# A 31-tap convolution rebuilt as column-tiled matmuls, its norm and the attention reordered ahead of a scan

## The reference, cut to what matters

```python
h = rms_norm(x, norm_mix_g); p = h @ w_in                       # (256, 2560)
q, pc, pr = split(p, [256, 256 + 768])
# cross attention to 256 memory rows, 4 heads of 64
s = einsum('qhd,mhd->hqm', q, mem_n @ w_mk) * 64 ** -0.5
o_att = einsum('hqm,mhd->qhd', softmax(s), mem_n @ w_mv)
# convolution: 384 channels, each with its own 31 taps along the tokens
val, gate = split(pc, 2)
u = conv(val * sigmoid(gate), conv_w, padding=15, groups=384) + conv_b
u = (u - mean(u)) * rsqrt(var(u) + 1e-5) * ln_g + ln_b          # over the 384 channels
o_conv = silu(u)
# RWKV: a scan in both directions over 6 heads of 64, in chunks of 32 tokens
y = scan_forward + scan_backward
y = (y - mean_head(y)) * rsqrt(var_head(y) + 64e-5) * lnx_g + lnx_b
o_rwkv = (y + sum_d sum_head(r * k_d * r_k) * v) * g            # the sum is the bonus
x = x + concat([o_att, o_conv, o_rwkv]) @ w_out                 # then 16 experts
```

## Time and profile before

| | |
|---|---|
| median of 3 runs | 1893.52 us |
| the profiled execution | 1893.73 us, its span 1891.9 us |
| PE busy, of the span | 1494.6 us (79%) |
| DVE, ACT, POOL busy | 464.9, 301.7, 95.1 us |
| the mixing stage, from its first matmul (h3T) to its last (output projection) | 1105.5 to 1376.8 us |
| of it, the scan | 1225.9 to 1333.7 us |
| the 16 experts and the end | 1377 to 1891.9 us |

### The profile page before, as it was taken

How to read it: one execution, slowest core, us unless ns; L and a number is a source line. 1 busy time by engine, 2 the same in 40 slices (tenths; PEclk the granted TensorE clock), 3 DMA queues, 4 the chain that set the end, 5 groups by cost and what they waited for, 6 DMA issues and landing times.

```text
span 1891.9 us, 25668 instructions
## 1 busy us (share of the span) xinstructions
PE 1494.6 (79%) x10943; PEld 850.7 (45%) x10943; DVE 464.9 (25%) x953; ACT 301.7 (16%) x666; POOL 95.1 (5%) x194
## 2 busy tenths in 40 slices
PE   6999988889896888888888769577857676766764
PEld 2845866778344343432343258366532131321321
DVE  1011234220016222212222253677530000000002
ACT  1101223440001111111111103221111010100100
POOL 3000021000000000000000000022000000000000
PEclk8999999889888899999999979677869798988978
DMA  9772362123664699999999772000238999999995
GB/s 353 166 262 80 112 223 95 55 79 112 226 244 156 280 428 428 429 430 427 429 430 427 303 269 91 0 3 4 90 144 356 429 428 427 430 428 428 429 429 231
DMA packets 84764, 510.29 MB, mean 270 GB/s; under 512 B 9527, under 2 KB 12376, under 8 KB 60118
## 3 DMA queue, kind: packets, MB, share of 16 engines
q1 hardware_dynamic: 80950, 500.21, 64.9%
q0 software_dynamic: 3744, 9.06, 2.1%
HBM read 506.10 MB, written 3.15 MB: 269 GB/s over the span
## 4 chain that ended last, share of the span: by engine, by line
PE 58%; DMA 24%; DVE 8%; issue 6%; ACT 3%; POOL 0%; SPq 0%; POOLq 0%; DVEq 0%; ACTq 0%; PEldq 0%
PE ps L1168 47%; DMA ring<-in_w_e_up 15%; DMA ring<-in_exp_w 7%; PE ps L1593 4%; PE ps L1730 3%; DVE hTs L2458 1%; DMA brow<-in_ada_b 1%; DMA ring<-in_ada_w 1%; DVE arena L2370 1%; PE ps L1578 1%; ACT arena L951 1%; DMA arena<-in_causal 1%; PE ps L1200 1%; ACT arena L941 1%; DVE stats L2058 0%
## 5 line engine op out<-in xcount | busy, mean ns | idle before, releaser
L1168 PE MATMUL ps<-ring,arena 128*32 128x512 f32 (+2 forms) x3492 | 483.0, 667 | 145.5 <-DMA ring<-in_w_e_up 81.8
L1168 PEld LDWEIGHTS ps<-ring,arena 128*32 128x32 f32 (+1 forms) x3492 | 133.4, 125 | 441.3 <-issue 376.0
L1168 PE MATMUL ps<-hTs,ring 128*128 128x256 f32 (+2 forms) x1120 | 249.9, 384 | 3.3 <-PE ps L1168 3.3
L1168 PEld LDWEIGHTS ps<-hTs,ring 128*128 128x128 f32 (+2 forms) x1120 | 210.9, 190 | 42.2 <-issue 11.5
L1168 PE MATMUL ps<-arena 128*128 (+5 forms) x576 | 139.5, 398 | 2.4 <-POOL arena L654 2.4
L1593 PE MATMUL ps<-arena 128*128 128x512 f32 x256 | 117.5, 601 | 29.0 <-DVE arena L2370 29.0
L1168 PEld LDWEIGHTS ps<-arena 128*128 128x128 f32 (+1 forms) x576 | 123.0, 294 | 18.9 <-issue 11.2
L1168 PE MATMUL ps<-ring,hTs 128*128 128x512 f32 (+2 forms) x288 | 106.2, 523 | 5.8 <-ACT hTs L1099 5.8
L1593 PEld LDWEIGHTS ps<-arena 128*128 128x128 f32 x256 | 46.0, 189 | 103.0 <-ACT arena L953 57.1
L2370 DVE COPY arena<-ps 128x512 f32<-128x512 f32 x32 | 22.1, 691 | 249.2 <-PE ps L1168 249.2
L2713 DVE TENSOR_TENSOR arena<-arena,ps 64x512 f32<-64x512 f32 x16 | 11.0, 690 | 292.1 <-ACT arena L1123 292.1
(11 more groups left out here) (423 smaller groups left out, 1235.1 us busy)
## 6 DMA issues: line engine op xcount, KB each, us to landing
ring<-in_exp_w SPq DMA_DIRECT2D x96, 2048.0 KB, 18.6
ring<-in_w_e_gate SPq DMA_DIRECT2D x32, 2048.0 KB, 18.8
ring<-in_w_e_up SPq DMA_DIRECT2D x32, 2048.0 KB, 23.3
ring<-in_w_e_down SPq DMA_DIRECT2D x32, 2048.0 KB, 24.0
ring<-in_w_in SPq DMA_DIRECT2D x22, 2048.0 KB, 14.1
ring<-in_ada_w SPq DMA_DIRECT2D x12, 2048.0 KB, 13.3
ring<-in_w_out SPq DMA_DIRECT2D x4, 2048.0 KB, 12.4
ring<-in_w_br_hg SPq DMA_DIRECT2D x2, 2048.0 KB, 15.4
```

The costliest lines, as they stand in the source:

```text
L1168: return nc.tensor.matmul(o, lhsT, rhs, start=start, stop=stop)
```

## The change

1. **Order of the projection.** The fourth weight tile (queries and two value groups) is kept, and the fifth (`in2b`, third value group and gates) goes first; what is left of the fourth comes behind `vt` as the jobs `ca` (values) and `qa` (queries), with the head sums of the bonus in between.
2. **Convolution on PE.** POOL multiplies `CU`, SP makes 16 DMAs from it into `lags`: the input of 32 channels in four copies, shifted by 0 to 3 tokens, on 128 partitions, for each of 12 groups. POOL builds `taps`, blocks of 128x32 with the taps on diagonals. A group is then 8 matmuls (shifts by 4) with 128x32 weights and 256 columns; four groups lie beside each other in one bank. The 93 DVE instructions go away.
3. **Its norm ahead of the scan.** ACT adds the bias while it empties the banks; the two channel sums `CM` and `CR` stand between the attention's jobs, POOL centres and squares, ACT takes the root, and DVE divides within the first pair of the scan, behind the four levels.
4. **Attention.** All four score jobs come first, each head has its own buffers; ACT's exponential reads the bank itself and scales by 0.125, and DVE only reduces and negates.
5. **Bonus** on POOL, straight after the low-rank results; `k_a` and `r_k` are folded into two column vectors by DVE.
6. **Behind the scan** PE goes to `gn1` at once, `project(0, 1)`, `gn2`, then `project(1, 5)`. ACT takes the root straight out of the bank with the epsilon as its bias. The scale and shift of the head norm are folded into `GG` and `BON` within the first pair, so that two products and one sum are left of it.

The diff, cut to its core:

```diff
-PLAN2 = [("h3T", 4), ("in2", 8), ("w0", 2), ("w1", 2), ("gg", 2), ("a0", 2), ("a1", 2),
-         ("kks", 2), ("vt", 2), ("in2b", 2), ("matt", 10), ("bon", 2), ("cmean", 1),
-         ("gn1", 2), ("y2", 4), ("cvar", 1), ("gn2", 2), ...
+PLAN2 = [("h3T", 4), ("in2", 6), ("in2b", 2), ("w0", 2), ("w1", 2), ("gg", 2), ("a0", 2), ("a1", 2),
+         ("kks", 2), ("vt", 2), ("ca", 1), ("bon", 2), ("qa", 1), ("matt", 14),
+         ("gn1", 2), ("y2", 4), ("gn2", 2), ...
-        ATT = ("S0", "S1", "T0", "S2", "T1", "O0", "S3", "T2", "T3", "O1")
+        ATT = ("S0", "S1", "S2", "S3", "C0", "C1", "T0", "T1", "CM", "T2", "O0", "T3", "CR", "O1")
@@ SP, ahead of the experts' first tiles
+            sp.wait_ge(S("cu_ready"), 1)
+            for j in range(4):
+                for q in range(4):
+                    sp.dma_start(lags[32 * j:32 * j + 32, q::4, :], CU[32 * q:32 * q + 32, :, j:j + 284])\
+                        .then_inc(S("lags_loaded"), 16)
@@ POOL
+            pool.wait_ge(freed[(N2 - 1) % RING], free_count(N2 - 1 - RING))
+            for j in range(4):
+                for q in range(4):
...
+                    ins = nc.gpsimd.tensor_copy(b, a)
...
+            for i, (o, n) in enumerate(((0, 40), (40, 56))):
+                ins = ptt(taps[i], mid(msk("eye32"), n), last(tapc[:, o:o + n], CHUNK), ALU.mult)
...
+            ptt(BON, AA[0], AA[1], ALU.add).then_inc(S("bonus_terms"), 1)
...
+            for c in range(3):
+                ins = nc.gpsimd.tensor_scalar(BON[:, c, :], BON[:, c, :], kark[:, c:c + 1], c2rk[:, c:c + 1],
+                                              ALU.mult, ALU.add)
...
+            ptt(BON, BON, K_, ALU.mult).then_inc(S("bonus_terms"), 1)
...
+            ptt(BON, BON, R_, ALU.mult).then_inc(S("bonus_terms"), 1)
...
+            is_out(pool, J("ca"))
+            all_out(pool, "in2b", 2)
+            ptt(CU[:, :, 15:271], CA, CS, ALU.mult).then_inc(S("cu_ready"), 1)
+            is_out(pool, jM("CM"))
+            ptt(CV, CV, mid(TMc, 3), ALU.subtract).then_inc(S("conv_centred"), 1)
+            pool.wait_ge(S("conv_centred"), 1)
+            ptt(CS, CV, CV, ALU.mult).then_inc(S("conv_centred"), 1)
@@ ACT
+            for h in range(4):
+                mexp(h)
...
+                    ins = nc.scalar.activation(CV[:, c, :], bank(jM(f"C{i}"))[:, (c % 2) * 256:(c % 2) * 256 + 256],
+                                               ACT.Identity, bias=col(1, VB["cb"] + c))
...
@@ PE
+            products(job("ca"), slot(n, (8, 512)), 256, hT)
+            pe.wait_ge(S("bonus_terms"), 4)
+            block_sums("bon", BON)
+            products(job("qa"), slot(n, (8, 512)), 0, hT)
...
+            def conv(c):
+
+                if c == 0:
+                    pe.wait_ge(S("taps_ready"), 2)
+                    pe.wait_ge(S("lags_loaded"), 256)
+                j = start(jM(f"C{c // 2}")) if c % 2 == 0 else jM("C0")
+                for s in range(8):
+                    for q in range(4):
+                        g = 4 * c + q
+                        ins = mm(bank(j)[32 * q:32 * q + 32, (c % 2) * 256:(c % 2) * 256 + 256], taps[g > 4][:, 8 * g + s - (40 if g > 4 else 0), :],
+                                 lags[:, g, 4 * s:4 * s + 256], s == 0, s == 7)
...
+            for h in range(4):
+                mscore(h)
+            for c in range(3):
+                conv(c)
+            mturn(0)
+            mturn(1)
+            is_out(pe, jM("C0"))
+            is_out(pe, jM("C1"))
+            channel_sums("CM", CV)
+            mturn(2)
+            mweigh(0)
+            mturn(3)
+            pe.wait_ge(S("conv_centred"), 2)
+            channel_sums("CR", CS)
+            mweigh(1)
...
-            channel_sums("cmean", CV, "tap_done", 93)
...
-            project(0, 2)
-            channel_sums("cvar", CS, "conv_centred")
+            project(0, 1)
             pe.wait_ge(S("gn_squares"), 1)
             block_sums("gn2", c3(3072))
             pe.wait_ge(S("conv_ready"), 1)
-            project(2, 5)
+            project(1, 5)
@@ DVE, in the scan's loop over p, behind the levels
-                convolve(6)
+                if p == 0:
+                    for c in range(3):
+                        ins = stt(BON[:, c, :], BON[:, c, :], col(1, VB["lxb"] + c), GG[:, c, :], ALU.add, ALU.mult)
+                    link(ins)
+                    is_out(dve, jM("CR"))
+                    link(nc.vector.reciprocal(CS[:, 0, :], CS[:, 0, :]))
+                    for c in range(3):
+                        ts(GG[:, c, :], GG[:, c, :], col(1, VB["lxg"] + c), None, ALU.mult)
+                    say(tt(CV, CV, mid(CS[:, 0, :], 3), ALU.mult), "conv_normed")
@@ DVE, behind the scan
+            link(tt(YY, YY, GG, ALU.mult))
+            all_out(dve, "gn2", 2)
             link(nc.vector.reciprocal(GS, GS))
             link(tt(YY, YY, GS, ALU.mult))
...
+            say(tt(MIX[:, 5:8, :], YY, BON, ALU.add), "mix_ready")
```

More of the change, by code:

```diff
@@ L63, in constants @@
         "mhalf": np.full((P, 1), -0.5),
+        "eps_conv": np.full((P, 1), 1e-5),
+        "eps_group": np.full((P, 1), 64e-5),
         "fold": (t[:, None] % 32 == np.arange(30)[None, :]),
@@ L411, in build @@
         wide = ((N2 - 1) % RING) * TILE + 2048
[L412 removed]
+        CU = ring[:, wide:wide + 3 * 288].rearrange("p (a b) -> p a b", a=3)
         PF = v3(AR[:, 0:3072], 12)
@@ L423, in build @@
         late4, late5 = ((N2 - 1 + k) % RING * TILE for k in (2, 3))
+        lags = ring[:, late4:late4 + 12 * 284].rearrange("p (g n) -> p g n", g=12)
+        tapc = AR[:, 20352:20448]
+        taps = [v3(a, n) for a, n in ((AR[:, 11904:13184], 40), (ring[:, wide - 1920:wide - 128], 56))]
         front = [AR[:, 8448:11136], ring[:, late5:late5 + 2688]]
@@ L985, in _ @@
             nc.scalar.activation(PF[:, 11, :], PF[:, 11, :], ACT.Sigmoid).then_inc(S("tanh_ready"), 1)
-            is_full(act, J("in2", 6))
-            frees(nc.scalar.copy(qa, v3(bank(J("in2", 6)), 2)), J("in2", 6))
-            is_full(act, J("in2", 7))
-            frees(nc.scalar.copy(CA[:, 0:2, :], v3(bank(J("in2", 7)), 2)), J("in2", 7))
+            b = [v3(bank(J("in2b", j)), 2) for j in range(2)]
+            is_full(act, J("in2b", 0))
+            nc.scalar.copy(CA[:, 2, :], b[0][:, 0, :])
+            frees(nc.scalar.activation(CS[:, 0, :], b[0][:, 1, :], ACT.Sigmoid), J("in2b", 0))
+            is_full(act, J("in2b", 1))
+            frees(nc.scalar.activation(CS[:, 1:3, :], b[1], ACT.Sigmoid), J("in2b", 1))
             def low_rank(name, dst, func, stack_col):
@@ L1029, in _ @@
             decays(0, 1)
-            b = [v3(bank(J("in2b", j)), 2) for j in range(2)]
-            is_full(act, J("in2b", 0))
-            nc.scalar.copy(CA[:, 2, :], b[0][:, 0, :])
-            frees(nc.scalar.activation(CS[:, 0, :], b[0][:, 1, :], ACT.Sigmoid), J("in2b", 0))
-            is_full(act, J("in2b", 1))
-            frees(nc.scalar.activation(CS[:, 1:3, :], b[1], ACT.Sigmoid), J("in2b", 1))
+            is_full(act, J("ca"))
+            frees(nc.scalar.copy(CA[:, 0:2, :], v3(bank(J("ca")), 2)), J("ca"))
+            is_full(act, J("qa"))
+            frees(nc.scalar.copy(qa, v3(bank(J("qa")), 2)), J("qa"))
             def mexp(h):
@@ L1050, in mout @@
                 frees(nc.scalar.copy(MIX[:, i, :], bank(jM(f"O{i}"), 256)), jM(f"O{i}"))
-            mexp(0)
-            mexp(1)
+            for h in range(4):
+                mexp(h)
+            for i in range(2):
+                is_full(act, jM(f"C{i}"))
+                for c in range(2 * i, min(3, 2 * i + 2)):
+                    ins = nc.scalar.activation(CV[:, c, :], bank(jM(f"C{i}"))[:, (c % 2) * 256:(c % 2) * 256 + 256],
+                                               ACT.Identity, bias=col(1, VB["cb"] + c))
+                frees(ins, jM(f"C{i}"))
             mcarry(0)
-            mexp(2)
             mcarry(1)
+            is_full(act, jM("CM"))
+            frees(nc.scalar.activation(TMc, bank(jM("CM"), 256), ACT.Copy, scale=1.0 / 384), jM("CM"))
+            mcarry(2)
             mout(0)
-            mexp(3)
-            mcarry(2)
             mcarry(3)
+            is_full(act, jM("CR"))
+            frees(nc.scalar.activation(CS[:, 0, :], bank(jM("CR"), 256), ACT.Sqrt, bias=C("eps_conv"),
+                                       scale=1.0 / 384), jM("CR"))
             mout(1)
@@ L1101, in _ @@
             ins.then_inc(S("conv_ready"), 1)
+            for i in range(2):
+                n = 2 - i
+                j = J("gn2", i)
+                is_full(act, j)
+                if i == 0:
+                    is_full(act, J("gn2", 1))
+                frees(nc.scalar.activation(c3(3072)[:, 2 * i:2 * i + n, :], v3(bank(j, 256 * n), n), ACT.Sqrt,
+                                           bias=C("eps_group"), scale=1.0 / 64), j)
             for j in (0, 2):
@@ L1646, in _ @@
             transposes("h3T", xn2)
-            for i in range(4):
+            for i in range(3):
                 n = tile("in2")
```

(14 more changed lines are left out.)

153 lines of the change are left out of this document (53 added, 100 removed).

## The result

| | before | after |
|---|---|---|
| median | 1892.91 us (1891.07 to 1895.28, 4 runs) | 1868.92 us (1867.21 to 1871.33, 4 runs) |
| ratio | | 0.987, 95% interval 0.9853 to 0.9886 |
| profiled execution, its span | 1893.73, 1891.9 us | 1867.28, 1865.3 us |
| PE, DVE, ACT, POOL busy | 1494.6, 464.9, 301.7, 95.1 us | 1476.8, 418.2, 302.9, 118.1 us |
| ahead of the scan (first transpose of the values to the scan's start) | 52.2 us | 47.9 us |

The change is faster by 24 us, against a forecast of 20.1. The three stretches gave 4.2, 9.2 and 12.7 us in the two profiles (26.1 together, 2 more than the medians), where the prediction had 6.9, 2.3 and 10.9.

The account below looks back on a forecast made before the run. Bound: the mixing stage and router, step after step, ahead of the expert weight stream at 1429 us. Gains of 10.9 + 2.3 + 6.9 = 20.1 us off the profiled 1893.73 give 1873.6 us, range 1866 to 1885.

Parts of the forecast that it names:

- Ahead of the scan: Attention, bonus and convolution before the scan: the scan starts at 1219, 6.9 us earlier, between 1215 and 1229.
- The price of the lock: POOL's bonus beside DVE's `prepare`: 3 us added to DVE (0 to 4.5) and 1 to POOL.
- the forecast by the rule alone: `prepare` on DVE: each of POOL's 7 us would be added to VectorE, so it would end at 1203.
- the forecast gap of 2.5 us: PE between scores and convolution: convolution starts at 1196.5, 2.5 us after the scores, and finds the clock up.
- Rival (a): Ahead of the scan: the 16 DMAs take 12 to 17 us instead of 10, scan near 1226, 1880 us; chance 0.14.
- In the scan: Taps removed from DVE, norm block added: gain 2 x 1.3 - 0.9 + 0.6 = 2.3 us, between -1 and 4.5.
- Behind the scan: Last result sum to last output projection matmul: 43.1 us becomes 32.2, gain 10.9 us, between 8.5 and 12.5.
- Rival (d): Expert stream: the gain ahead of it is eaten there, as that stage waits for transfers; about 1893 us; chance 0.04.
- (b): Ahead of the scan: transfer at the 8-partition row's price, `lags` at 1226, scan at 1251, 1905 us; chance 0.05.
- the five signs of being right: PE idle under 4 us, convolution 11 us, scan at 1219, gapless 32 us tail, experts 20 us earlier.
- the case that I gave 0.57: Whole kernel: the measured time lies within 4 us of 1873.6 us; chance 0.57.
- the one that I gave 0.10: Whole kernel: more gained, since PE stays at full clock into the scan, 1864 to 1869 us; chance 0.10.

Follow-up runs that it names:

- the values first: The changed kernel with ACT copying the value groups out of their bank ahead of the second direction's exponentials: 1869.6 us, ratio 0.9839.
- the version with two queues: The changed kernel with the value groups copied earlier and ACT issuing 8 of the 16 shifted copies beside SP: 1872.5 us, ratio 0.9855.

## Why the prediction held, and where its terms were off

**Ahead of the scan: forecast 6.9, measured 4.2 us.** The price of the lock was right: DVE lost 3.5 us (3 forecast) and `prepare` ended at 1199.4 (1199). The bonus was there at 1181.6 (1182), and the convolution's input at 1187.3 (1186.5). The Trainium skill's rule, page "SBUF — State Buffer", section "SBUF: two separate sides", gives the direction, since three scans beside POOL took four times as long; but DVE lost 3.5 us beside 8 us of POOL's work, so the forecast by the rule alone, an end of `prepare` at 1203, didn't come.

Two terms were mis-sized. An issue was priced at 0.47 us, from one plain load; these take 10.45 / 16 = 0.65. That is 3 us more, and with the 0.8 us of the input the last copy is there at 1199.4 and not at 1196.5. The second term is what follows: at the forecast gap of 2.5 us I let the clock stand, at 6.4 us it fell, and the convolution took 13.4 us and not 10.9. The gap itself was summed wrongly: 1182 + 1.3 + 7.0 + 2.3 is 1192.6 and not 1194, and PE was through at 1193.1. So the forecast's own terms give a gap of 3.9 us, and with the values first a gap of 3.2 us was enough for the clock to fall. The convolution ended 4.9 us late, at 1212.9. The steps behind it made up for 2.3 of these: the scan began 8.7 us after it, where I had counted 11 (the terms add up to 10.4). Rival (a), a late transfer, is what happened, 12.1 us from the first issue to the last landing, at less than half its price. No run takes back the attention's new order or the convolution on PE alone, so how the 4.2 us divide between them isn't shown.

**In the scan: forecast 2.3, measured 9.2 us,** outside its range of -1 to 4.5. The place was right, the last level of each pair beside POOL's products. The term was mis-sized: it held only the 1.3 us of waiting per pair. In the cut above, in the changed kernel's order, 3 us go per pair, part of them PE's own work at the lower clock, 6 of the taps' 6.8 us. Of the rest of the 9.2, some is favour: the changed kernel's scan of 98.6 us is the shortest of the eight that it and its variants without taps have, whose mean is 100.8. By that mean the gain is 6.8 us (107.6 less 100.8), and the stretches sum to 23.7, beside the 24.0 of the medians. The new norm block did make PE wait, 1.7 us for 0.9 forecast. In the first pair of the kernel before PE waits three times 0.5 us for ACT's copies, in four of four profiles of that kernel and of its version without taps; in the changed kernel one such wait of 0.4 us is left. It may be why that version's first pair stays over 51 us. I have not tried it alone.

**Behind the scan: forecast 10.9, measured 12.7 us,** just outside its range (8.5 to 12.5), by the clock again. No run takes back a part of this stretch alone, so what follows is read from the profiles. I had PE at half clock through `gn1` and part of `project(0, 1)`. Windows of the version with the bonus on DVE, where it was so:

```profile
1314.00:1317.00 3.00, 2.91 (x7) 2.40 (x8) 0.00 (x0) 1.32 (x3) 0.00 (x0) 0.50 0.70 213
1317.00:1322.00 5.00, 5.00 (x9) 2.05 (x9) 3.03 (x4) 0.00 (x0) 0.00 (x0) 0.70 1.03 442
```

There the stretch takes 34.2 us. In the kernel after the clock rose within the scan's last six us and was full at `gn1` (the windows at the top), and it takes 31.25. Five of the variants have 31.2 to 31.3 us, and there too the clock rose ahead of the scan's last sum; four have 32.7 to 34.2, with the clock at half for three to six us behind it. Nothing waited behind gn2, as forecast: the chain has 30.31 us in one piece.

**The stream.** It took the whole gain: the experts started 26.4 us earlier, and what follows the stage has the same length within 0.6 us (514.3 and 513.8). Rival (d) is out, and (b) too: a copy of 106 KB from 32 partitions lands in 2.2 us.

The clock had a part in all three errors, once against the forecast and twice in its favour, beside the price of an issue and the idle time per pair. The errors, -2.7, +6.9 and +1.8 in the profiles, partly cancelled, and the median came out 4.7 us below the forecast. That the sum came so close is luck in part: of the five signs of being right three failed (the gap of 6.4 us, the convolution of 13.4, the scan's start at 1221.7), and 1868.9 us lies not in the case that I gave 0.57 but at the edge of the one that I gave 0.10, a clock that stays up into the scan. It did stay up, to 1232, but the clock of the kernel before was also full from 1226 to 1238, so that is not what the scan gained.

## What to carry to other kernels

Price a wait of PE together with the clock that it may cost on the work behind it: here a wait priced at 1.3 us cost 3, and a gap of 6.4 us cost 2.8 more. Work on another engine that is "hidden" is so only if the engine's next step for the critical one is not queued behind it; look for the one tap or copy that stands in front of it while a neighbour engine slows both. Before splitting a batch of transfers over two queues, look at what stands behind them in the first.

## What I had not expected of the hardware

- The same instructions of the scan took 98.6 to 103.5 us in six profiles of kernels that have it alike, at granted clocks between 0.69 and 0.78 in its pairs. PE has 6 to 13 us of idle time in each pair that nothing in the profile explains ("issue").
- One copy of 106.5 KB within SBUF lands in 2.2 us, 16 in a row from one queue go at 0.65 us each and some 165 GB/s, and two queues together reach some 250 (1188 to 1192 us of the version with two queues); beside a 2 MB load the last of them took 9.9 us.
- Three scans of 128x128 with two inputs in SBUF took 4.30 us beside POOL's products of 768 elements and 1.05 us without.
